# Dilated attention in six rounds instead of three, with its transposes in the scores' banks and first halves of three output units between

## The reference, cut to what matters

```
for g, (window, dilation) in enumerate(((128, 1), (512, 4), (2048, 16))):
    o, lse = dilated_group_attention(q[:, :, g], k[:, :, g], v[:, :, g], window, dilation)   # 4 heads of 64
wts = softmax(stack(lse), axis=0)
y_att = einsum("gbsh,gbshd->bshd", wts, stack(o))                 # 256 tokens x 256
x = x + concatenate([y_lru, y_att], axis=-1) @ w_out              # 768 -> 1024
h = rmsnorm(x, ffn_norm_g);  x = x + conv_glu_ffn(h, ...)
```

## Time and profile before

| | us |
|---|---|
| runs shown, median (lowest to highest) | 1691.41 (1680.44 to 1691.9) |
| profiled execution, its own time | 1685.43 |
| its span, first to last instruction | 1683.6 |
| TensorE busy in the span | 1619.7 |
| VectorE, ScalarE, GpSimd busy | 1280.9, 859.1, 62.1 |
| mean granted clock of TensorE, as a share of full speed | 0.988 |

### The profile page before, as it was taken

One profiled execution on the slowest core, in us unless ns is written; L12 is line 12 of the kernel. 1 busy time (PEld: TensorE's weight loads), 2 busy tenths in 40 slices (PEclk: granted clock), 3 DMA queues, 4 the chain that ended last, 5 costly groups with the idle time before them and its releaser, 6 DMA issues.

```text
span 1683.6 us, 27026 instructions
## 1 busy us (share of the span) xinstructions
PE 1619.7 (96%) x11073; PEld 1465.0 (87%) x11073; DVE 1280.9 (76%) x1450; ACT 859.1 (51%) x1024; POOL 62.1 (4%) x69
## 2 busy tenths in 40 slices
PE   6998999999899999999999999999999999999997
PEld 6988999887689999899998699998899988799996
DVE  7868889878858897778888577885788877585554
ACT  5565645555356555644455364444644455455453
POOL 3001000000000000100000010000000010000000
PEclk9999999999899999999999899999999999999998
DMA  7514888643236875489854248975598944155550
GB/s 240 176 51 144 294 309 299 228 154 113 91 94 238 318 280 194 150 305 316 304 193 154 82 144 295 312 249 175 181 321 300 320 133 156 47 190 192 182 191 33
DMA packets 230944, 342.81 MB, mean 204 GB/s; under 512 B 7010, under 2 KB 194000, under 8 KB 230864
## 3 DMA queue, kind: packets, MB, share of 16 engines
q1 hardware_dynamic: 229888, 340.64, 59.9%
q0 software_dynamic: 672, 0.79, 0.2%
q10 hardware_dynamic: 304, 0.27, 0.1%
HBM read 340.62 MB, written 1.05 MB: 203 GB/s over the span
## 4 chain that ended last, share of the span: by engine, by line
PE 76%; DVE 13%; issue 4%; ACT 4%; POOL 1%; DMA 0%; DVEq 0%; ACTq 0%
PE PS L628 20%; PE PS L715 19%; PE PS L629 10%; PE PS L608 7%; PE PS L587 6%; DVE wl L1422 4%; PE PS L595 3%; PE PS L653 2%; PE PS L694 2%; PE PS L767 2%; PE PS L836 2%; DVE Z L1523 1%; ACT wh L1012 1%; DVE RS L1868 1%; PE PS L669 1%
## 5 line engine op out<-in xcount | busy, mean ns | idle before, releaser
L1422 DVE TENSOR_TENSOR wl<-raw,wh 128x2048 fp32r<-128x2048 f32 (+2 forms) x257 | 575.5, 2243 | 151.1 <-ACT wh L1012 149.2
L628 PE MATMUL PS<-HP,wh 128*128 128x512 f32 x1728 | 607.9, 395 | 0.2 <-DVE wl L1422 0.2
L1012 ACT ACTIVATE wh<-raw 128x2048 fp32r<-128x2048 f32 (+2 forms) x257 | 477.5, 1860 | 137.9 <-PE PS L715 118.1
L629 PE MATMUL PS<-HP,wl 128*128 128x256 f32 x1728 | 484.1, 280 | 0.0
L628 PEld LDWEIGHTS PS<-HP,wh 128*128 128x128 f32 x1728 | 324.1, 188 | 75.0 <-DVE wl L1422 0.5
L715 PE MATMUL PS<-FX,wh 128*128 128x256 f32 x1920 | 344.8, 281 | 1.8 <-DVE FX L1589 1.8
L629 PEld LDWEIGHTS PS<-HP,wl 128*128 128x128 f32 x1728 | 326.3, 189 | 0.0
L715 PEld LDWEIGHTS PS<-FX,wh 128*128 128x128 f32 x1920 | 294.7, 188 | 4.4 <-DVE wl L1422 2.0
L715 PE MATMUL PS<-FX,wl 128*128 128x256 f32 x960 | 269.9, 281 | 0.0
L715 PEld LDWEIGHTS PS<-FX,wl 128*128 128x128 f32 x960 | 180.6, 188 | 0.0
L587 PE MATMUL PS<-FX,wh 128*128 128x258 f32 (+2 forms) x576 | 145.1, 290 | 20.9 <-ACT FX L1024 10.3
(11 more groups left out here) (259 smaller groups left out, 1790.1 us busy)
## 6 DMA issues: line engine op xcount, KB each, us to landing
ada<-ada_w SPq DMA_DIRECT2D x144, 512.0 KB, 6.3
raw<-ffn_w_gate SPq DMA_DIRECT2D x66, 1024.0 KB, 5.4
raw<-ffn_w_up SPq DMA_DIRECT2D x66, 1024.0 KB, 5.4
raw<-ffn_w_down SPq DMA_DIRECT2D x66, 1024.0 KB, 5.3
raw<-od_w_in SPq DMA_DIRECT2D x13, 1024.0 KB, 5.3
raw<-ev_w_in SPq DMA_DIRECT2D x10, 1024.0 KB, 7.8
raw<-w_in SPq DMA_DIRECT2D x8, 1024.0 KB, 5.4
raw<-w_out SPq DMA_DIRECT2D x8, 1024.0 KB, 6.3
```

The source lines that it names most:

```text
L628: mm(pairs(bank(bk)), lhsT=lhs(0, k), rhs=HP[:, k], start=k == 0, stop=False, skip_group_check=True)
L629: last = mm(bank(bk, 0, S), lhsT=lhs(1, k), rhs=HH[:, k, :], start=False, stop=k == k_tiles - 1, skip_group_check=True)
L1012: last = A_(dst(wh), src, ACT.Copy)
L1422: last = tt(dst(wl), src, dst(wh).bitcast(F32), ALU.subtract)
```

## The change

Six rounds of 768 columns each take the place of three: block 0 with heads 0 and 1, then 2 and 3; block 1 with one head each. Scores alternate between banks 0 and 1 and banks 2 and 3 (`s`), and the transposes go back into the same two banks (`pt`), so `scores(r)` now waits for the copy `turned(r-2)`. Probabilities have four places in SBUF (`S`), transposed ones two (`PT`), and each round writes its own part of bank 7. The dummy matmuls are gone from the stage. In their place TensorE issues the first halves (chunks 0 and 1, 24 matmuls) of output units 0, 1 and 2, into banks 4, 5 and 6: one between scores(0) and scores(1), one behind turn(0), one behind turn(1). Their second halves (12 matmuls each) and unit 3 in bank 7 follow the last values. `fill` of chunks 0 and 1 moves ahead: on ScalarE before exps(0), on VectorE between masked(0) and masked(1). VectorE runs masked(r+2) behind probs(r).

```diff
-            for r, (b, heads) in enumerate(((0, (0, 1, 2, 3)), (1, (0, 1)), (1, (2, 3)))):
+            for r, (b, heads) in enumerate(((0, (0, 1)), (0, (2, 3)), (1, (0,)), (1, (1,)), (1, (2,)), (1, (3,)))):
...
-                out.append({"b": b, "heads": heads, "w": w, "s": 0, "ns": 3, "pt": 3, "o": 7, "scores": sc,
-                            "values": va, "S": (r % 2) * 1536, "PT": 3072, "scale": 1.0,
-                            "masks": [(0, 3 * nk * P, m)]})
+                out.append({"b": b, "heads": heads, "w": w, "s": 2 * (r % 2), "ns": 2, "pt": 2 * (r % 2), "scores": sc,
+                            "values": va, "S": (r % 4) * 768, "PT": 3072 + 768 * (r % 2), "scale": 1.0, "S_sets": 4,
+                            "PT_sets": 2})
...
-            def half_unit(n, bk, fill, second):
+            def half_unit(n, bk, fill, second, k_tiles=KD):
-                w = weights(n, KD)
+                w = weights(n, k_tiles)
                 for m in range(2):
-                    for k in range(4 * second, 4 * second + 4):
+                    for k in range(4 * second, min(4 * second + 4, k_tiles)):
...
-                    if r and rd["s"] == rounds[r - 1]["s"]:
-                        pe.wait_ge(ev(st + "_masked"), l * R + r)
+                    if r >= 2:
+                        pe.wait_ge(ev(st + "_turned"), l * R + r - 1)
...
-            spin(5, 6)
+            half_unit(od, 4, fill, False, 6)
             scores(1)
-            turn(0)
-            scores(2)
...
+            for r in range(6):
+                turn(r)
+                if r < 2:
+                    half_unit(od + 1 + r, 5 + r, fill, False, 6)
+                if r < 4:
+                    scores(r + 2)
+                values(r)
+            for u in range(3):
+                half_unit(od + u, 4 + u, fill, True, 6)
+            project(od + 3, 7, k_tiles=6)
...
+            fill((0, 1), ready)
+            exps(0)
+            exps(1)
+            for r in range(6):
+                turned(r)
+                if r < 4:
+                    exps(r + 2)
+                taken(r)
+            fill((2,), ready)
...
+            masked(0)
+            fill("y_od", (0, 1), ready)
+            masked(1)
+            for r in range(6):
+                probs(r)
+                if r < 4:
+                    masked(r + 2)
+            fill("y_od", (2,), ready)
+            out_units(U0["od_out"], "ffn1", ffnn1, first=4)
```

More of the change, by code:

```diff
@@ L391, in dilated_rounds @@
                             chain.append((v, (i * w) // P + g * nk + kb))
-                    va.append((PS[half, 7, (h // 2) * P:(h // 2 + 1) * P], chain))
+                    va.append((PS[half, 7, 256 * b + (h // 2) * P:256 * b + (h // 2 + 1) * P], chain))
                 sc.sort(key=lambda e: (e[0] // w) % 2)
-                m = mask[:, :, P:2 * P] if b == 0 else mask
-                out.append({"b": b, "heads": heads, "w": w, "s": 0, "ns": 3, "pt": 3, "o": 7, "scores": sc,
-                            "values": va, "S": (r % 2) * 1536, "PT": 3072, "scale": 1.0,
-                            "masks": [(0, 3 * nk * P, m)]})
+                out.append({"b": b, "heads": heads, "w": w, "s": 2 * (r % 2), "ns": 2, "pt": 2 * (r % 2), "scores": sc,
+                            "values": va, "S": (r % 4) * 768, "PT": 3072 + 768 * (r % 2), "scale": 1.0, "S_sets": 4,
+                            "PT_sets": 2})
             return out
@@ L417, in latent_rounds @@
                             "scores": sc, "values": va, "S": (0, 512)[b], "PT": (3072, 3584)[b],
-                            "scale": (HN + HR) ** -0.5})
+                            "scale": (HN + HR) ** -0.5, "S_sets": 2, "PT_sets": 2})
             return out
@@ L757, in scores @@
                     rd = rounds[r]
-                    if r and rd["s"] == rounds[r - 1]["s"]:
-                        pe.wait_ge(ev(st + "_masked"), l * R + r)
+                    if r >= 2:
+                        pe.wait_ge(ev(st + "_turned"), l * R + r - 1)
                     flat = banks(rd["s"], rd["ns"])
                     for at, (dst, parts) in enumerate(rd["scores"]):
-                        if at == len(rd["scores"]) // 2:
+                        if at == len(rd["scores"]) // 2 and len(rd["heads"]) > 1:
                             last.then_inc(ev(st + "_even"), 1)
-                            pe.wait_ge(ev(st + "_even"), l * R + r + 1)
+                            pe.wait_ge(ev(st + "_even"), 2 * l + r + 1)
                         for i, (q, k) in enumerate(parts):
@@ L784, in values @@
                     pe.wait_ge(ev(st + "_turned"), l * R + r + 1)
-                    if r and rd["o"] == rounds[r - 1]["o"]:
-                        pe.wait_ge(ev(st + "_taken"), l * R + r)
                     for dst, chain in rd["values"]:
@@ L887, in _ @@
             pe.wait_ge(z_out, 22)
+            od, fill = U0["od_out"], "y_od"
             scores(0)
-            spin(5, 6)
+            half_unit(od, 4, fill, False, 6)
             scores(1)
-            turn(0)
-            scores(2)
-            spin(4, 6)
-            values(0)
-            spin(3, 6)
-            turn(1)
-            spin(4, 6)
-            values(1)
-            turn(2)
-            spin(4, 6)
-            values(2)
-            for u in range(4):
-                project(U0["od_out"] + u, u, k_tiles=6, fill="y_od" if u == 0 else None)
+            for r in range(6):
[8 more added lines that the diff above has]
+            project(od + 3, 7, k_tiles=6)
             ffn(1, "ffn1")
@@ L1142, in turned @@
                     act.wait_ge(ev(st + "_pt"), l * R + r + 1)
-                    if r and rd["PT"] == rounds[r - 1]["PT"]:
-                        act.wait_ge(ev(st + "_o"), l * R + r)
+                    if r >= rd["PT_sets"]:
+                        act.wait_ge(ev(st + "_o"), l * R + r + 1 - rd["PT_sets"])
                     n = rd["w"] * len(rd["heads"])
@@ L1293, in taken @@
                 act.wait_ge(ev("dil_o"), r + 1)
-                t = rd["heads"][0] // 2
-                n = len(rd["heads"]) // 2
-                A_(T[:, 4 + t:4 + t + n, rd["b"] * P:(rd["b"] + 1) * P],
-                   PS[:, 7, t * P:(t + n) * P].rearrange("p (t s) -> p t s", s=P), ACT.Copy).then_inc(ev("dil_taken"), 1)
-            exps(0)
-            turned(0)
-            exps(1)
-            taken(0)
-            turned(1)
-            exps(2)
-            taken(1)
-            turned(2)
-            taken(2)
+                b, h = rd["b"], rd["heads"][0]
+                half = slice(0, P) if len(rd["heads"]) > 1 else slice(64 * (h % 2), 64 * (h % 2) + 64)
+                A_(T[half, 4 + h // 2, b * P:(b + 1) * P],
+                   PS[half, 7, 256 * b + (h // 2) * P:256 * b + (h // 2 + 1) * P], ACT.Copy).then_inc(ev("dil_taken"), 1)
             def ready(c):
@@ L1312, in ready @@
                 else:
-                    act.wait_ge(ev("dil_taken"), 3)
-            fill(range(3), ready)
+                    act.wait_ge(ev("dil_taken"), 6)
+            fill((0, 1), ready)
[7 more added lines that the diff above has]
+            fill((2,), ready)
             out_units(U0["od_out"], "ffn1", lambda t: pc("ffnn1", t))
@@ L1623, in masked @@
                     dve.wait_ge(ev(st + "_scores"), l * R + r + 1)
-                    if r >= 2:
-                        dve.wait_ge(ev(st + "_pt"), l * R + r - 1)
+                    if r >= rd["S_sets"]:
+                        dve.wait_ge(ev(st + "_pt"), l * R + r + 1 - rd["S_sets"])
                     flat = banks(rd["s"], rd["ns"])[:, 0:c]
@@ L1923, in ready @@
                 else:
-                    dve.wait_ge(ev("dil_taken"), 3)
-            fill("y_od", range(3), ready)
-            out_units(U0["od_out"], "ffn1", ffnn1)
+                    dve.wait_ge(ev("dil_taken"), 6)
+            masked(0)
[7 more added lines that the diff above has]
+            out_units(U0["od_out"], "ffn1", ffnn1, first=4)
             chain = norm("ffn1", ffnn1, deferred=U0["ffn1"] + 2)
```

6 lines of the change are left out of this document (removed).

## The result

The changed kernel takes 1712.4 us (median of five executions, 1702.27 to 1713.9) against 1691.14 (1680.44 to 1691.9) for the kernel before: the ratio is 1.015, with a 95% interval of 1.0119 to 1.018. It is slower by 21 us. Two later sets of executions, on other occasions, gave 1.0108 (1.0053 to 1.0164) and 1.0139 (1.0097 to 1.0182).

A forecast was written before the change was run, and what follows sets the result against it. The attention stage was taken as bound by its serial ring across engines, none saturated. Order at full clock +8.0, clock +4.5, +3.3 and +1.2 gave +17.0 on 1685.4, so 1702.4 us; range 1690 to 1713.

The forecast's parts named there:

- Start: From masking 0: first half unit waits for VectorE's low part, scores 1 follow it; scaling 0 ends 452.85 at full clock.
- Rounds 0 and 1: First two loop rounds: 8.3 and 8.1 us, to 469.28 for scaling 2, with each half unit on the path.
- Rounds 2 and 3: Later rounds without half units: scores r+2 wait for the copy out of their banks; 6.3 us each, to 481.88.
- Tail: Last transposes, copies, values and operand parts after the rounds: left operand's last third complete at 489.4.
- What is bought: Output stage: 14.7 us against 19.93, bound by VectorE's splits; 5.2 of the 8.8 us moved ahead are gained.
- Clock of the half units: Attention stage: gaps before each half unit drop TensorE to half clock; three times 1.5, +4.5 us.
- Clock of rounds 2 to 5 and of the output stage: Half clock in both places: half of 6.6, so +3.3 us, in the rounds; +1.2 of 3.3 in the output stage.
- The bound and the base: Sum made on the profiled 1685.43 us; one per cent, 17 us, taken as what measurement can tell from no change.
- Rival 1: TensorE's clock stays up or returns within each half unit: +8.0 with up to 4 more, 1693 to 1698; chance 0.23.
- Rival 2: Attention rounds overlap and VectorE becomes the bound: -15.4, or -14 with a cold half unit, 1670 to 1672; chance 0.05.
- Rival 3: Clock low nearly throughout, all clock bounds at their upper end: +22.4, 1707.8, up to 1714; chance 0.20.
- Rival 4: Output stage bound by TensorE, not VectorE's splits: about 11 us, delay 3.8 smaller, 1698.6; chance 0.05.

The follow-up runs named there:

- second profile: The changed kernel, unedited, profiled again beside follow-up runs; the profiled execution took 1711.97 us.
- the third: The changed kernel, unedited, profiled a third time; the profiled execution took 1699.75 us.
- e1: Changed kernel with the scores of round 1 issued ahead of the first half unit instead of behind it; 1699.39 us, ratio 1.007 to the kernel before.
- e3: e1 with the second and third half units also moved behind the scores of round r+2; 1698.06 us, ratio 1.006 to the kernel before.
- e5: Changed kernel without half units, transposes in banks 4 and 5, scores r+2 ahead of transposes r, values one round later; 1688.28 us, ratio 1.0015 to before.
- e7: e5 with one half unit between scores(1) and the loop, in place of its four dummy matmuls; 1681.6 us, ratio 0.9964 to the kernel before.
- e10: e9 with a second half unit, the first half of output unit 1, behind values(5); 1677.76 us, ratio 0.9965 to the kernel before.
- e9: e7 with four dummy matmuls ahead of the half unit; 1682.75 us, ratio 0.9991 to the kernel before.

## Why the prediction was right or wrong, point by point

Forecast was +17.0 us, with no measurable change as the likelier outcome (0.52) on a bound of 17; measured were +21.3, +20.8 and +22.0 on the medians, which is slower. The order of events came out as described; two things failed, the size given to the clock and the reading of the sum against the bound. The time, 1712.4, lies inside the range, and on the profiled executions the difference is 1702.27 - 1685.43 = +16.84. That this is so near the sum's +17.0 is luck: 2.8 us of it arose ahead of the stretch, where the kernels are alike, 14.9 in it, and 0.9 were regained behind it. The second profile would have given +19.9 in the stretch, the third +15.1.

- **Start: right.** From the beginning of masking 0 to the end of scaling 0 were 10.7 us plus 1.5 for the clock, 12.2; measured 12.1 (13.4 in the second profile, whose first half unit took 5.46 us). TensorE was idle 4.15 us in front of the first half unit, with VectorE's low part as the releaser.
- **Rounds 0 and 1: right.** 8.3 + 8.1 plus 3.0 for the clock is 19.4; measured to the end of scaling 2, 19.5 (18.9 in the second profile). The half unit stands on the path each time, as e1 and e3 confirm.
- **Rounds 2 and 3: right in order.** 12.6 at full clock; measured 14.2, with the scores of round 4 at 2.92 us instead of 1.56. The copy out of the shared banks is on the ring, as e5 confirms.
- **Tail: right in order, priced 0.9 short.** 7.5 predicted, 8.4 measured, at full clock. The values were put at 1.20 and 1.36 us and took 1.52 and 1.54; the high part was put at 0.55 and took 0.64.
- **What is bought: right.** Output stage 14.7 predicted, 14.78 and 14.66 measured, 0.56 us of waiting for unit 3's split, and an idle gap of 3.56 us ahead of the last quarter, in this timeline of TensorE of the changed kernel:

```profile
504.29 0.50 PE L607 MATMUL PS<-HP,wh 128*128 128x256 f32 x2 [0.56 <-DVE wl L1415]
...
513.87 0.38 PE L586 MATMUL PS<-FX,wh 128*128 128x256 f32 x1 [3.56 <-ACT FX L1019]
```

- **Clock of the half units: right.** +4.5 for three; they took 4.4, 4.1 and 4.4 us in the chain against 2.9 to 3.0, and 5.5, 4.7 and 2.9 in the second profile, nearly the same sum.
- **Clock of rounds 2 to 5 and of the output stage: the term that was mis-sized.** "I take half, 3.3" and "I take 1.2 of 3.3" give one value to a term that differs from execution to execution. Against the same steps at full clock (12.6 and 8.35), rounds 2 to 5 lost 1.6 us to the clock in the first profile, 1.7 in the third and 4.3 in the second; the output stage and what follows lost 0, 0 and 1.6. So the 4.5 us taken were too many for the two quick executions and 1.4 too few for the slow one, which also lost 1.1 more at the start. The second profile is the one nearest to the usual execution in its time: 1711.97 us, where four of the first five took 1712.26 to 1713.9; its mean granted clock is lower than theirs, 0.972 against 0.975 to 0.977, and the first profile's is 0.985. I had weighed the values, which held the clock at 471.97, against the scores, which did not; in the new order scores at half clock go straight over into values, and these stay at half clock in the second profile (2.82 us instead of 1.52).
- **The bound and the base: the step that failed in reading the sum.** "One per cent, 17 us, is about what a measurement of this kernel can tell from no change" has no run behind it. The measured interval, 1.0119 to 1.018 from five executions, is 5 us to either side, and 7 to 9 us in the two later sets, so the sum's own +17.0 would have counted as slower. I also made the sum against an execution near the lower end, which left 6 us to the range; 1712.4 lies inside that range by 0.6 us.
- **Rivals.** Rival 1 (clock back within each half unit) fell with the 4.4 us half units. Rival 2 (rounds overlap) is not what the changed kernel does; e5 and e7 show that its mechanism works once the transposes have banks of their own, but the best version that has it, e10, came out 5 us below the kernel before, where I had priced the overlap at 14 to 15. Rival 3 (+22.4) comes nearest to the medians, but its condition, a clock low nearly throughout, was met in no profile: the slowest lost 5.9 of the 9.9 us of its bounds. Rival 4 fell with the gap of 3.56 us.

**What is shown and what is not.** Shown by experiment: the place of the half units (8.5 us of stretch) and the shared banks with the order they force (7.4 to 11.8 of stretch). Less firmly shown is the clock (8 on the medians, with overlapping intervals). These overlap and do not add up to the 21. Open: the profiles differ by 17.6 us in the mean stretch and the medians by 21, so some 4 us of a usual execution stand in no mean of profiles; that the unprofiled executions are like the second profile is inferred from their time and mean clock. Nor do the runs show what sends the clock down in one execution and not in the next.

## What to carry to other kernels

Work that is to fill an engine's gap must stand behind everything that another engine waits for, or it makes the ring longer by as much of its own length as nothing hides: the same three half units cost at least 3.8 us where they stood. With banks of their own for the transposes, one half unit made the stretch 2.7 us shorter and two made it 5.5 shorter, clock included, although the first still delayed scores 2. Cutting rounds in half paid only where two could be under way at once, and then by itself it merely drew level (e5); so give each intermediate result banks of its own before cutting rounds. And when a sum ends on the bound between two answers, look first at how far the executions already measured lie apart, and give a term that varies with the clock two values, one for each kind of execution.

## What the runs showed of the hardware that was not expected

A busy TensorE did not keep its clock: in e5 it was busy 20.08 of 21.00 us at a granted clock of 0.51, with four dummy matmuls and otherwise float32 scores, transposes and values, and it rose only at 465. In e10, busy 18.70 of 22.90 us with the same kinds of instruction, it stayed at 1.00 from 451 on:

```profile
451.00:473.90 22.90, 18.70 (x131) 14.71 (x129) 12.12 (x24) 10.31 (x23) 0.00 (x0) 1.00 0.01 4
```

e9 is e5 with one half unit of output matmuls behind the same dummy matmuls, and there the clock was up again at 448.8 and stayed up for the rounds. So the half unit ahead of the rounds is what differs; but each of these is one profile, and the changed kernel, with three half units, fell to half clock again in rounds 2 to 5. Second, a slower execution of one kernel had a lower mean granted clock: the changed kernel took 1699.75 us at 0.986, 1702.27 at 0.985 and 1712.87 at 0.977; the kernel before 1680.37 at 0.986 and 1694.67 at 0.977. Third, the same time at half clock costs more or less by where it falls: the kernel before had 13.7 us of it in and behind the attention stage in three profiles, and its stretch was 156.8 in two of them and 159.6 in the other.
